# Moving a layer norm and the joining of experts' rows from feature-major to token rows

## What is computed

```python
for l in range(2):
    ...                                             # mixer: attention, convolution, gating, @ w_out
    ctx = layer_norm(ALPHA * ctx + mod_c[2] * o_c, ln1_g, ln1_b)     # layer 0 only
    x = layer_norm(ALPHA * x + g1 * o_x, ln1_g, ln1_b)
    tokens = x * (1 + sc2) + sh2                    # and the same for ctx in layer 0
    y = hier_moe(tokens, ...)                       # router: 4 groups x 8 experts, top 2 of one group
    x = layer_norm(ALPHA * x + g2 * y, ln2_g, ln2_b)                 # and ctx in layer 0
```

## Time and profile before

| | us |
|---|---|
| median of 3 runs | 2997.12 |
| lowest and highest run | 2990.25, 2999.2 |
| span of the profiled execution | 2997.1 |
| PE busy | 2632.2 (88%) |
| DVE busy | 1313.0 (44%) |
| ACT busy | 650.1 (22%) |
| POOL busy | 522.4 (17%) |

### The profile page before, as it was taken

One profiled execution on the slowest core, in us unless ns is written; L12 is line 12 of the kernel. 1 busy time (PEld: TensorE's weight loads), 2 busy tenths in 40 slices (PEclk: granted clock), 3 DMA queues, 4 the chain that ended last, 5 costly groups with the idle time before them and its releaser, 6 DMA issues. The chain is left out here.

```text
span 2997.1 us, 45567 instructions
## 1 busy us (share of the span) xinstructions
PE 2632.2 (88%) x17218; PEld 1772.2 (59%) x17219; DVE 1313.0 (44%) x2527; ACT 650.1 (22%) x1344; POOL 522.4 (17%) x537
## 2 busy tenths in 40 slices
PE   7999989999999998989958998989788884898765
PEld 6877766488885484557545554545567752455333
DVE  6752367248999932447361111111435733222114
ACT  3540168120100011027131000000222531111002
POOL 3432012014440000310201100000122201121101
PEclk9999999999999999989988999999899996999877
DMA  4232320138555632021028889999712125999994
GB/s 143 92 123 65 138 78 26 57 97 230 199 197 213 260 136 69 0 102 47 29 77 350 355 352 421 412 413 374 262 50 89 60 91 223 363 383 381 407 421 153
DMA packets 137324, 594.64 MB, mean 198 GB/s; under 512 B 20337, under 2 KB 40589, under 8 KB 90609
## 3 DMA queue, kind: packets, MB, share of 16 engines
q1 hardware_dynamic: 86704, 359.25, 31.6%
q10 hardware_dynamic: 41808, 212.75, 17.7%
q0 software_dynamic: 8688, 21.00, 2.0%
HBM read 574.06 MB, written 33.69 MB: 203 GB/s over the span
## 5 line engine op out<-in xcount | busy, mean ns | idle before, releaser
L1440 DVE SCALAR_TENSOR_TENSOR psum<-weight_ring,condition_rows 128x1024 f32<-128x1024 f32 x192 | 268.1, 1397 | 16.0 <-issue 0.9
L2980 DVE COPY expert_hidden_turned<-psum 128x128 f32<-128x128 f32 (+1 forms) x93 | 32.6, 351 | 462.5 <-PE psum L2838 462.5
L268 PE MATMUL psum<-weight_ring 128*128 128x256 f32 (+1 forms) x896 | 221.9, 398 | 3.0 <-POOL weight_ring L253 3.0
L2827 PE MATMUL psum<-weight_ring,slot_rows_turned 128*32 128x256 f32 x2176 | 147.3, 417 | 74.9 <-DMA weight_ring<-in_w_dram 43.4
L2816 PE MATMUL psum<-weight_ring,slot_rows_turned 128*64 128x256 f32 x1792 | 205.5, 383 | 0.5 <-issue 0.5
L268 PEld LDWEIGHTS psum<-weight_ring 128*128 128x128 f32 x896 | 170.6, 191 | 43.1 <-issue 4.3
L2908 ACT ACTIVATE expert_silu<-psum 64x256 f32<-64x256 f32 (+1 forms) x91 | 34.6, 380 | 657.4 <-PE psum L2816 349.8
L2816 PEld LDWEIGHTS psum<-weight_ring,slot_rows_turned 128*64 128x64 f32 x1792 | 127.3, 138 | 76.4 <-issue 16.9
L2845 PE MATMUL psum<-weight_ring,expert_hidden_turned 128*32 128x256 f32 (+1 forms) x1536 | 165.8, 441 | 0.0
L2966 DVE TENSOR_TENSOR expert_hidden<-expert_silu,psum 64x256 f32<-64x256 f32 (+1 forms) x93 | 39.2, 422 | 276.8 <-ACT expert_silu L2908 254.6
L174 PE MATMUL psum<-ffn_hidden,weight_ring 128*128 128x512 f32 (+1 forms) x440 | 154.3, 514 | 4.1 <-DVE ffn_hidden L1485 4.1
(11 more groups left out here) (501 smaller groups left out, 4682.3 us busy)
## 6 DMA issues: line engine op xcount, KB each, us to landing
third_stream_weights<-in_w_dram ACTq DMA_DIRECT2D x93, 2048.0 KB, 14.5
weight_ring<-in_w_dram SPq DMA_DIRECT2D x84, 2048.0 KB, 17.9
weight_ring<-in_w_ada_dram SPq DMA_DIRECT2D x24, 2048.0 KB, 8.5
weight_ring<-in_w_ffn_dram SPq DMA_DIRECT2D x11, 2048.0 KB, 12.4
weight_ring<-in_w_rnn_dram SPq DMA_DIRECT2D x8, 1536.0 KB, 6.5
weight_ring<-in_w_att_dram SPq DMA_DIRECT2D x6, 2048.0 KB, 8.0
weight_ring<-in_w_in_dram SPq DMA_DIRECT2D x6, 2048.0 KB, 11.2
weight_ring<-in_w_down_dram SPq DMA_DIRECT2D x8, 1408.0 KB, 6.1
```

Source lines behind the costliest of these rows:

```text
L268: last = c.nc.tensor.matmul(to, weights[:, k * P:(k + 1) * P], rhs[:, k], start=(starts and k == 0), stop=(stops and k == KH - 1), skip_gr ...
L1440: last = v.scalar_tensor_tensor(out=product, in0=w[:, t], scalar=1.0, in1=CR[:, n, :], op0=ALU.mult, op1=ALU.mult, accum_out=c.mod[:, i // ...
L2827: last = nc.tensor.matmul(ps[units.rows(2 * m + o), 2 + b, 0:256], XT[:, b, k % tiles, units.rows(k // tiles)], w[:, k, 256 * o:256 * (o + ...
L2980: v.tensor_copy(HT[:, b, :, :], ps[:, 1, 0:256].rearrange("p (k s) -> p k s", k=2)[:, :, 0:2 * cap])\
```

## The change

- `layer_norm` no longer writes to `X` in feature layout. PE turns each 128 tokens of `X` (three ahead), DVE takes mean and variance of the rows from PSUM with two bn_stats and a bn_aggr, ACT takes the root, DVE makes scale and shift, ACT writes the normed rows to `XR` (in the place of the later `mix2`, or `normed_rows` in layer 1). The logits are made from un-normed `X` as stationary operand, with router weights that POOL has multiplied by the modulation (`WS`, 288 columns, 4 or 2 instructions), and are corrected by sums of these weights.
- The modulated token rows that the experts gather are made by POOL in `route`: two multiplies and two additions of `[128, 512]` for each 128 tokens, between clearing the slots and the first gathers. SP stores them there.
- The rows' modulation vectors come from a new DRAM table, which `modulate` writes once (ACT, PE, SP) and which SP loads with a broadcast to all partitions (`MOD`, 16 KB per partition; `R.affine`; `GATES`).
- In `experts` POOL multiplies the rows by ALPHA times the gain and adds the bias, four `[128, 512]` instructions for each 128 tokens, after the third gather of the loop. ACT's eight instructions on `X` (2925) go. Work buffers of the experts lie in `X`, which is free then.
- `combine_and_norm` joins in rows: DVE adds the second choice, multiplies by the gate row, adds to `XR`, and takes bn_stats; ACT normalises the row; PE turns it; ACT (for the last pair half DVE) writes out of PSUM. In layer 0 DVE also copies the normed 512 tokens to `X`. The gathers go to six-slot ring buffers without waiting for each other; four ring slots are refilled only after all rows are summed.
- Gains that used to be applied in the norm are folded into the modulation (six short DVE instructions in the first block's tail, and a pointer in place of ALPHA in line 2216).

The mean and variance matmuls are gone; the turns come first and the logits are short matmuls with 36 columns. The core of the diff:

```diff
-def layer_norm(c, n, gain, modulated, router):
+def layer_norm(c, l, nt, router, XR):
...
+                g.memset(router.ONES[:, :], 1.0)
+                router.consts.wait(pool, 16 * 5)
+                for v in range(nv):
+                    for n, at in enumerate((32, 24)):
+                        by = c.mod[:, l, at:at + KT, v].unsqueeze(2).broadcast_to([P, KT, RW])
+                        g.tensor_tensor(WS[:, :, v, n, :], router.WR[:, :, :], by, ALU.mult).then_inc(router_scaled.sem, 1)
...
+                for t in range(3):
+                    turn(t)
+                router_scaled.wait(pe, 2 * nv)
+                for k in range(KT):
+                    last = nc.tensor.matmul(ps[:, 7, 0:nv * 2 * RW], router.ONES[:, :],
+                                            WS[:, k, :, :, :].rearrange("p v n w -> p (v n w)"),
+                                            start=(k == 0), stop=(k == KT - 1))
+                last.then_inc(sums_ready.sem, 1)
+                for t in range(nt):
+                    if t + 3 < nt:
+                        turn(t + 3)
+                    logit(t)
...
             @block.gpsimd
             def _(pool):
-                nc.gpsimd.memset(R.rows[:, :, :], 0.0)
+                nc.gpsimd.memset(R.rows, 0.0)
+                router.rows_in.wait(pool, 16)
+                split = units_of.groups // 2
+                for t in range(nt):
+                    v, row = 0 if t < ST else 1, router.ROW[:, t % 3, :]
+                    if t >= 3:
+                        router.stored[t % 3].wait(pool, 16 * (t // 3))
+                    for h in range(2):
...
+                        out = row[:, at].rearrange("p (c a e) -> p a c e", c=split, e=4 // split)
+                        nc.gpsimd.tensor_tensor(out, turned(XR(t)), turned(router.MOD[:, SCALE_ROW + v, :]), ALU.mult)
+                    pool.drain()
...
+                        last = nc.gpsimd.tensor_tensor(out, out, turned(router.MOD[:, SHIFT_ROW + v, :]), ALU.add)
+                    last.then_inc(router.made.sem, 1)
                 pool.drain()
                 for b in range(3):
                     router.stored[b].wait(pool, 16 * len(range(b, nt, 3)))
                 placed.wait(pool, 3)
...
+                last = rounds(pool)
+                for b in range(NSTREAM):
+                    gather(0, b)
+                for t in range(nt):
+                    for h in range(2):
+                        x = XR(t)[:, h * D // 2:(h + 1) * D // 2]
+                        nc.gpsimd.tensor_tensor(x, x, R.affine[h], ALU.mult)
+                        pool.drain()
+                        nc.gpsimd.tensor_tensor(x, x, R.affine[2 + h], ALU.add)
+                with pool.Fori(1, last) as it:
                     for b in range(NSTREAM):
...
-                for k in range(KT):
-                    x = c.X[:, k, 0:nt * P]
-                    nc.scalar.activation(x, x, ACT.Identity, scale=ALPHA, bias=c.vec(f"ln1_b{l}", k))
...
+            @block.vector
+            def _(dve):
...
+                for i in range(nt):
+                    y = choice(0, i)
                     weighted.wait(dve, i + 1)
+                    v.scalar_tensor_tensor(out=y, in0=choice(1, i), scalar=R.gate[:, 1, i:i + 1], in1=y,
+                                           op0=ALU.mult, op1=ALU.add)
                     dve.drain()
+                    v.tensor_tensor(y, y, gate_of(i), ALU.mult)
+                    if i >= 1:
+                        finish(i - 1)
+                    dve.drain()
+                    v.tensor_tensor(XR(i), XR(i), y, ALU.add).then_inc(summed.sem, 1)
+                    dve.drain()
+                    for h in range(2):
+                        v.bn_stats(BN[:, i, h, :], XR(i)[:, h * D // 2:(h + 1) * D // 2])
+                    dve.drain()
+                    v.bn_aggr(MV[:, i, :], BN[:, i, :, :].rearrange("p h n -> p (h n)")).then_inc(stats_ready.sem, 1)
+                    if i % per == 1 and i // per - 1 in copies:
+                        p = i // per - 1
+                        out_act.wait(dve, p + 1)
+                        v.tensor_copy(X[:, :, cols(p)], whole(p)).then_inc(out_dve.sem, 1)
```

625 lines of the change are left out of this document (312 added, 313 removed).

## The result

| | before | after |
|---|---|---|
| median, us | 2995.81 (4 runs) | 3010.94 (4 runs) |
| lowest and highest | 2990.25, 2999.2 | 3009.11, 3015.98 |
| span of the profiled execution | 2997.1 | 3014.2 |
| ratio of times | | 1.0048 (95%: 1.0034 to 1.0062) |

The changed kernel is slower by 15.1 us, clearly more than the noise. The forecast was 3001.0 with a range of 2977 to 3019: the range held the time, but the likeliest case (no measurable change) did not come, and 11 of the 15 us are missing from the sum. The profiled execution of after is the slowest of its four, so single stages are compared first, and totals by the medians. The forecast column sets each term of the sum beside its stretch.

A forecast was written before the change was run, and what follows sets the result against it. It saw PE full in the large stages and six short stages (266.8 of 2997.1 us) bound by chains between engines; -11.8 - 9.7 + 18.8 + 13.4 + 3 - 8.4 - 1.4 = +3.9 gave 3001.0 us, range 2977 to 3019.

The forecast's parts named there:

- the likeliest case: Whole kernel: no measurable change in time, chance 0.44, against 0.34 for slower and 0.22 for faster.
- The 32.2 us of the sum: `route`: DVE's chain to `slot_index` delayed by POOL's instructions, +18.8 us in layer 0 and +13.4 in layer 1.
- two narrow rows: L572 and L576: 8 columns, 1.22 and 1.27 us beside POOL, not 0.17; read as turns by whole instruction.
- the walk: `route`: DVE's old instruction list stepped against POOL's; 27 lose 0.7 us in layer 0, 21 lose 0.64 in layer 1.
- Rival 1: `route`: narrow DVE instructions do not wait for POOL; routing costs some 3 us a layer, time 2974.8; chance 0.17.
- Rival 2: `route`: POOL slower on rows it writes, in layer 1 (3008.6 us) or both layers (3019.8); chance 0.25.
- the step that failed: Layer 1's first norm: 88 PE records at 0.125 us plus 1 for the clock's return, norm -9.7 us.
- rival 3: Norms: short logit matmuls at PE's lower clock throughout; 3012.8 us with layer 0, 3022 with layer 1; chance 0.06.
- The prediction's own sign to watch: Norms: the prediction called itself wrong if the logits take over 3 us a tile.
- The restart at 1513.2: Layer 0's norm: PE gets on once loads land at 1510 and POOL's four scalings take 3.2 us; norm -11.8.
- Forecast +3: Layer 0's experts: POOL's 24 instructions delay its next gather and PE stalls 5 us, partly regained: +3 (0 to 8).
- Joining: Joining the experts' rows: DVE's row pace and waits behind ACT's writes give -8.4 us in layer 1, -1.4 in layer 0.

The follow-up runs named there:

- the quarters: Changed kernel with every POOL row instruction in `route` cut into four of 128 columns: 3007.53 us (1.0036).
- the seven traces: Traces with the experts' scaling in one piece and the same rows: layer 0's experts took 544.1 to 548.2 us, 545.6 in the mean.
- the four with the scaling spread: Traces with POOL's scaling in layer 0's experts spread two instructions behind each next gather: that stage 541.7 to 542.5 us; spreading alone on the changed kernel, 3012.24 us.
- the filler experiment: Changed kernel with 56 more PE turns of 128x128 while PE waits for the scaled router weights: 3004.01 us (1.0025).
- the last version: Second all-together version (2969.18 us) plus 5 and 11 filler PE turns between the sums and the fourth turn: 2968.24 us (0.9906).

## Why the prediction was right, and what it missed

**Routing, right.** The 32.2 us of the sum are 32.8 in the trace. The reading that carried it was of two narrow rows, and the run without POOL's arithmetic and the quarters show its mechanism and not its size alone. The closeness of the size is partly luck: the walk had 27 instructions lose 0.7 us each in layer 0 and 21 lose 0.64 in layer 1; set beside those of the kernel before one by one, 23 lose 0.88 and 16 lose 0.88. The products are right because fewer instructions lost more each. Rival 1 (narrow instructions slip through) is out by the 1.22 of line 2562. Rival 2 (POOL slower on the rows it writes) is out by medians of 1.26 in layer 0 and 1.28 in layer 1.

**Norm, layer 1: the step that failed.** The prediction took PE on 10.6 us into the stage; it was 10.3. It then gave 88 records 0.125 each "plus 1 for PE coming back from idle". They took 18.9 us, 6.9 more than the 12; a tail of 1.2 for 2.1 and the earlier start took 1.3 of that back, so the norm gave -4.1 for -9.7. That was rival 3, which got a chance of 0.06 on the ground that "in a dense run PE came back to its full clock within one long instruction group before". The prediction names no row for it, and behind this wait PE did not come back, though it was never idle again. Filling PE's wait, with nothing else changed, gave back 7.1 us, so the term that failed is the clock behind the wait. The rival's price for this layer, 9 us (3012.8 to 3022), was of the right kind and 2 too high; that it struck one layer and not both was nowhere foreseen, and why PE came back in layer 0 stays open. The prediction's own sign to watch, over 3 us a tile for the logits, came: 3.4.

**Norm, layer 0.** The restart at 1513.2 was right (0.85 later in a trace that began 0.85 later), through errors that cancel, which is luck: the last load took 4.4 us and not 3.5, but was issued 0.3 sooner into the stage, and POOL's four took 2.6 and not 3.2. The records took 20.1 us for 18, the tail 1.3 for 2.1: -10.5 for -11.8. What the step did not ask is why POOL's loads should come that late at all; loading its two of the five a stage earlier gave 10 and 13 us.

**Experts.** Forecast +3. The trace says +5.4, the seven traces +3.1 and the four with the scaling spread -0.4, so the price of the piece is some 3.5; that the forecast's +3 meets the mean to 0.1 means little in a stage that varies by 4 us from trace to trace. POOL was free 57.9 us after the stage's first turn (forecast 57.7), and PE's seventh turn slipped by 4.1 where 5 were forecast.

**Joining.** Layer 1's tile on DVE takes 5.74 (5.7), the wait behind ACT's writes 1.89 (1.8); small gaps add up to 1.1. In layer 0 the pace gained 0.8 of 1.4, and the gathers' delay (1.7 in this trace, about 1.1 in the mean of all) was missed: the prediction costed the change's new gate load at nothing and named no cover for it.

**Together:** the terms with the experts' mean instead of their one trace, -10.5 + 19.4 + 3.1 + 1.0 - 4.1 + 13.4 - 7.3, are +15.0, and the medians differ by 15.1. Of the 11 us missing, 6.9 are the two norms and 3.5 the joinings. The direction was left open at 0.34 for slower; the largest single piece of what decided it, 6.9 us, came from the rival with the lowest chance, in layer 1. That the time still fell within the range is due to the range's width, which other rivals had set, and not to the sum.

## What to carry to other kernels

Before work is given to an idle POOL, look at what DVE does beside it: here a chain of short DVE instructions, nearly all with two SBUF operands, lost up to one whole POOL instruction (0.9 us on average) at each that met one, so the price goes by the length of POOL's instructions and the number of DVE's, not by the size of DVE's; shorten POOL's (which halved the loss in layer 1, but made POOL itself the late one in layer 0), or put them beside DVE work from PSUM. A small load that an engine waits for should be issued a stage early, ahead of the large ones, because the wait costs twice when PE idles behind it. And where short matmuls follow a wait, price them at both clocks. With early weights, rows made partly in the norm, quarters in `route` and the scaling spread in layer 0, the change is worth having: 2968 to 2969 us, 0.9% below the kernel before.

## What the runs showed of the hardware

- A run of 36-column matmuls did not keep PE's clock: at 1.00 and never idle, it fell to 0.50 within the run (windows of the filler experiment), and did the same in layer 0 of the changed kernel, where the clock of 1526.0 to 1534.7 is 0.76 in the mean, and in the last version (0.61 for 2434 to 2436).
- After the same wait of 1.37 us the clock was 1.00 in one trace and 0.50 in another, 9.0 and 13.7 us for 64 records. With the same code for layer 1's norm the clock stayed at 0.50 behind the wait in four traces (13.71 us for 64 records) and came back in one (10.59).
- The same load took 6.4 to 7.2 us behind 2 MB on its own queue and 13.4 to 13.7 on another queue beside them. Loaded a stage earlier, ahead of the weights, it took 2.4.
- A POOL multiply or add took 1.26 us for 512 columns, 0.67 for 288, and 0.42 to 0.45 for 128 in `route`.
- A DVE reduce with one SBUF operand ran its 0.35 us undisturbed inside a POOL instruction, and DVE's work from PSUM in `experts` took the same with POOL beside it as without (0.692 for 0.691); instructions of 32 to 192 columns with two SBUF operands, and a TENSOR_SCALAR of 24 with one, waited.
